# Attention over cached pages: plain float32 matmuls in column quarters in place of split operands

## Chip, cores and metric

The kernel runs on one core of a Trainium2 chip. The metric is the device time of one execution in microseconds (us), lower is better.

## The reference

One inference step of a two-layer decoder: layer 0 is a causal pooling mixer, layer 1 an attention with forget gates. It runs for a prompt (1 x 1024 rows) and for 8 sample sequences of 4 new rows with 2048 past rows in a paged cache (16 pages of 128 rows each). Width 1024, 16 heads of 64. The part that matters here is the sample group's attention:

```python
k_all = jnp.concatenate([past[0], k_new], axis=1)      # 2048 cached rows + 4 new
v_all = jnp.concatenate([past[1], v_new], axis=1)
F_all = jnp.cumsum(lf_all, axis=1)
s = jnp.einsum('bqhd,bkhd->bhqk', q, k_all) * (HEAD_DIM ** -0.5)
s = s + (fq[..., :, None] - fk[..., None, :])          # forget bias, per head
s = jnp.where(mask, s, NEG)
p = jax.nn.softmax(s, axis=-1)
o = jnp.einsum('bhqk,bkhd->bqhd', p, v_all)
```

Everything is float32.

## The kernel before

`build` runs stages with a barrier between them: conditioning, pooling, two output and residual stages, projections, then `stage_attention` (from L1130), and an output and residual stage. Only `stage_attention` changes. In it each engine has its own program, and semaphores order them.

**Steps.** TensorE, ScalarE, VectorE and GpSimd all loop over `for s in range(STEPS)`, with 151 steps. Three streams of work run side by side in a step:
- Prompt attention, one unit a step for steps 0 to 127: one head and one block of 128 queries (`scores` L1394, `turn_probs` L1407, `values` L1414), with VectorE's `logits`, `row_max`, `normalise` and ScalarE's `exps` between. The number of key blocks, 1 to 8, alternates short and long.
- Pages of K, one a step for steps 0 to 127: `turn_K` (L1423) transposes a page of 128 rows in 8 transposes to PSUM banks 6 and 7. Every second step `page_scores` (L1432) takes two pages. A batch has 16 pages, so 8 batches take 128 steps.
- Pages of V, one a step from step V0 = 22 on, to step 149: `page_values` (L1452). The last 22 pages are a tail in which the other two streams have ended.

Side work (`side`, L1471) comes once a batch of 16 steps at fixed steps (`side_work` L1210, L1201): prompt output transposes, transposes of the sample probabilities (`PTd`, `PTn`), and the transposes of the sample output. It uses bank 6 as `turn_K` does, so the next `turn_K` waits until it is read.

**Splits.** A plain float32 matmul costs TensorE more passes than one on fp32r data, so K, V, the queries and the probabilities of the cached pages are split into a high part (cast to fp32r) and the rest. K is split on its way out of PSUM: ScalarE casts (L1561), VectorE subtracts (L1694). V is split in SBUF: ScalarE casts (L1555), GpSimd or, late, VectorE subtracts (L1276). The 64 rows of a batch (16 heads x 4 queries) stand twice in the 128 stationary columns, high and low:

```python
pe.matmul(out, E_all[:, bq, :], G[:, 2 * g * P:2 * (g + 1) * P], start=True, stop=False)
for c in range(NP):
    for kt in (KTh, KTl):
        mm = pe.matmul(out, qst[:, bq % 2, c * P:(c + 1) * P], kt[:, j % 2, c, :], ...)
```

The first matmul (L1440) adds the forget bias `G` by a selector. ScalarE then copies the low rows (L1548) and VectorE adds both halves (L1673). Output bank 3 is shared with `values`, so `page_scores` and `values` wait for each other's readers (L1513, L1522). For V the same is done in L1465 to L1468, with 512 columns a matmul, into banks 4 and 5; L1486 sums and transposes the result by `J`.

**Loads.** SP issues all loads in one list sorted by due time (L1246): pages of K into a ring of 3, of V into a ring of 2 (at the end also into the buffers of K), and for each pair of heads of the prompt qT, kT, zT and Vt. SP waits in order.

**Start.** GpSimd clears and builds masks (L1334 to L1361), VectorE computes the cumulated forget values (L1627) and `G` (L1630); TensorE's first step waits for `newT` and `nmask` (L1501).

Of the kernel before, what the change touches and what calls it, by code (L numbers as in the profile page):

```python
# [59 lines left out]
KR = 3  # L60
VR = 2
# [72 lines left out]
def build(nc, x_prompt, x_sample, state_pool, cache_k, cache_v, cache_logf, page_table, c_prompt,  # L134
# [53 lines left out]
    negF_d = scratch("negF_d", (NH, SEQ))  # L188

# [940 lines left out]
    def stage_attention():  # L1130
# [7 lines left out]
        KTh = a.take("KTh", [P, 2, NP, 2 * P], F32R)  # L1138
        KTl = a.take("KTl", [P, 2, NP, 2 * P], F32R)
        KT_end = a.at  # L1140
        Vh = a.take("Vh", [P, VR, D], F32R)
        Vl = a.take("Vl", [P, VR, D], F32R)
# [20 lines left out]
        QW = P + 2 * NT  # L1163
        qst = a.take("qst", [P, 2, NP * QW], F32R)
        newT = a.take("newT", [NS, NB, NP, 2 * NT])
        Sd = a.take("Sd", [NR, 2, PAST + NS])
        Slo = a.take("Slo", [NR, 2 * P])
        PTd = a.take("PTd", [P, NPG, 2 * NR], F32R)
        PTn = a.take("PTn", [NS, 2 * NR])
        O_sb = a.take("O_sb", [P, D])  # L1170
        J = a.take("J", [P, 3 * NR])
        E_all = a.take("E_all", [P, NB, P])
        G = a.take("Gf", [P, PAST + NS])
        nmask = a.take("nmask", [NR, 2 * NS - NT])
        dstat = a.take("dstat", [NR, 2, 4])
        zero = a.take("zero", [P, 1])
# [14 lines left out]
        mpre = b.take("mpre", [NR, NH, 2 * NS - NT])  # L1191
# [9 lines left out]
        G_OUT, G_PTD, G_PTN, G_PTD2, G_OS = (2, 3), 4, 5, 7, 6  # L1201
# [8 lines left out]
        def side_work(s):  # L1210
# [6 lines left out]
            if g in (G_PTD, G_PTN, G_PTD2) and r < NB:  # L1217
                return "probs", r, (G_PTD, G_PTN, G_PTD2).index(g)
# [9 lines left out]
        s_VK = [sem(f"s_VK{i}") for i in range(KR)]  # L1228
# [5 lines left out]
        s_Kt, s_Kh, s_Kl, s_sc, s_Slo, s_rowe = (sem(n) for n in ("s_Kt", "s_Kh", "s_Kl", "s_sc", "s_Slo", "s_rowe"))  # L1234
        s_Vh, s_Vl = sem("s_Vh"), [sem(f"s_Vl{i}") for i in range(VR)]
        s_qs, s_side_hi, s_ogd = sem("s_qs"), sem("s_side_hi"), [sem(f"s_ogd{i}") for i in range(2)]
# [16 lines left out]
        for p in range(NP):  # L1253
            loads.append((UN * p + 3.8 if p else -9.0, "nF", 2 * p + 1))
        loads.sort()

        TAIL = PAGES - V0
        rest = [(K, x % KR) for x in range(PAGES - KR, PAGES)] + [(V, (TAIL + x) % VR) for x in range(VR)]  # L1260
        places, last, landed = [], {("K", x % KR): ("K", x) for x in range(PAGES - KR, PAGES)}, {}
        for t in range(PAGES):
            buf, i = (V, t % VR) if t < TAIL else rest[(t - TAIL) % len(rest)]
            key = ("K" if buf is K else "V", i)
            landed[key] = landed.get(key, 0) + 16
            places.append((buf[:, i], s_V[i] if buf is V else s_VK[i], landed[key], last.get(key)))
            last[key] = ("V", t)

        def dve_splits(t):

            return t + V0 - 1 >= NU

        def V_low(eng, t):

            eng.wait_ge(s_Vh, t + 1)
            eng.tensor_tensor(Vl[:, t % VR], places[t][0], Vh[:, t % VR].bitcast(F32), ALU.subtract).then_inc(  # L1276
                s_Vl[t % VR], 1)

        with nc.Block() as block:
            @block.sync  # L1280
            def _(sp):
                def pair_loads(p):
# [8 lines left out]
                    sp.dma_start(Vt[:, i], vp[:, :, p * P:(p + 1) * P]).then_inc(s_pair[i], 16)  # L1291

# [17 lines left out]
                for _, what, t in loads:  # L1310
                    if what == "pair":
                        pair_loads(t)
                    elif what == "nF":
                        head_load(t)
                    elif what == "K":
                        if t >= KR:
# [473 lines left out]
```

## Time and profile before

| what | us |
|---|---|
| median of 3 runs | 2380.86 |
| lowest, highest | 2380.86, 2383.38 |
| span of the profiled execution | 2378.0 |
| attention stage in it, first unit's step to last page value | 1379 to 2211 |

The profiled execution's own device time is not given beside its span; its instructions fill 2378.0 us, and the median of the runs is 2.9 us above that. In the rows further down PE is TensorE's matmul, PEld its weight load, DVE VectorE, ACT ScalarE, POOL GpSimd, SPq the queue of SyncE. "L1443" is a line of the kernel before, "x8" a count. A record is one instruction as the trace has it; the ends of matmuls are modelled, so that distances between starts say more than durations.

### The profile page before, as it was taken

The numbers are of one execution on the slowest core, as the hardware profiler recorded it, in microseconds if no ns is written. First come the engines' busy times: TensorE is split into PE (matmuls) and PEld (weight loads), VectorE is DVE, ScalarE is ACT, GpSimd is POOL, SyncE is SP. The second block draws the span as 40 slices with busy tenths as digits, with TensorE's granted clock in tenths as the row PEclk, the third lists the DMA queues.
The fourth block names the chain that finished last, engine by engine and source line by source line (L and its number), as shares of the span: only waits on it lengthen the run. The fifth ranks groups of instructions, "written<-read, shape, count | busy, mean of one in ns | idle before, by whom it ended". The sixth has DMA issues, their size and how long they took to land. (4 is left out here: it accounts for less than half of the span.)

```text
span 2378.0 us, 33033 instructions
## 1 busy us (share of the span) xinstructions
PE 2125.1 (89%) x12939; PEld 1865.5 (78%) x12939; DVE 906.3 (38%) x1510; ACT 763.2 (32%) x1459; POOL 693.5 (29%) x512
## 2 busy tenths in 40 slices
PE   6969999999799924999999889999999999997692
PEld 1269999999799913999999867778788787876692
DVE  1332333344310066210000166555665655655305
ACT  2111111111212133100001135666666656655332
POOL 0123222333122214222233200444444444441122
PEclk9989999999899955999999889999999999999896
DMA  8621212121421041343333243665656656555404
GB/s 282 220 71 40 83 48 82 49 81 50 175 88 45 18 166 30 110 112 93 84 99 97 87 165 119 227 220 186 213 184 226 213 193 213 187 184 189 143 20 166
DMA packets 231052, 312.81 MB, mean 132 GB/s; under 512 B 39777, under 2 KB 165330, under 8 KB 230779
## 3 DMA queue, kind: packets, MB, share of 16 engines
q1 hardware_dynamic: 199251, 266.13, 34.9%
q10 hardware_dynamic: 31520, 44.50, 5.3%
q8 instruction: 103, 1.69, 0.3%
q14 instruction: 50, 0.41, 0.1%
q0 software_dynamic: 128, 0.07, 0.0%
HBM read 266.09 MB, written 44.57 MB: 131 GB/s over the span
## 5 line engine op out<-in xcount | busy, mean ns | idle before, releaser
L1276 POOL TENSOR_TENSOR Vl<-V,Vh 128x1024 fp32r<-128x1024 f32 x106 | 251.9, 2377 | 2.5 <-ACT Vh L1555 2.5
L121 PE MATMUL ps<-actH,w_hi_a 128*128 128x352 f32 x960 | 210.4, 327 | 3.4 <-DVE w_lo_a L92 3.4
L121 PE MATMUL ps<-actH,w_lo_a 128*128 128x352 f32 x960 | 207.8, 324 | 0.0
L121 PE MATMUL ps<-actL,w_hi_a 128*128 128x352 f32 x960 | 207.4, 324 | 0.0
L121 PE MATMUL ps<-actH,w_hi_c 128*128 128x352 f32 x792 | 173.3, 327 | 20.9 <-DVE w_lo_c L92 20.9
L1694 DVE TENSOR_TENSOR KTl<-ps,KTh 128x512 fp32r<-128x512 f32 x256 | 164.5, 685 | 54.3 <-ACT KTh L1561 52.7
L121 PE MATMUL ps<-actH,w_lo_c 128*128 128x352 f32 x792 | 171.5, 324 | 0.0
L121 PE MATMUL ps<-actL,w_hi_c 128*128 128x352 f32 x792 | 171.4, 325 | 0.0
L121 PEld LDWEIGHTS ps<-actH,w_hi_a 128*128 128x128 f32 x960 | 163.4, 190 | 3.8 <-DVE w_lo_a L92 3.7
L1561 ACT CAST KTh<-ps 128x512 fp32r<-128x512 f32 x256 | 137.4, 588 | 89.5 <-PE ps L1428 86.9
L121 PEld LDWEIGHTS ps<-actH,w_lo_a 128*128 128x128 f32 x960 | 165.5, 189 | 0.0
L121 PEld LDWEIGHTS ps<-actL,w_hi_a 128*128 128x128 f32 x960 | 163.7, 189 | 0.0
L1403 PE MATMUL ps<-kT,qT 64*128 64x512 f32 (+3 forms) x384 | 159.6, 523 | 4.1 <-DMA Vt<-out_dram 1.7
L1428 PEld LDWEIGHTS ps<-ident,K 128*128 128x128 f32 x1024 | 111.6, 142 | 64.5 <-issue 44.2
L121 PEld LDWEIGHTS ps<-actH,w_hi_c 128*128 128x128 f32 x792 | 134.8, 190 | 21.0 <-DVE w_lo_c L92 21.0
L1428 PE MATMUL ps<-ident,K 128*128 128x128 f32 x1024 | 142.3, 283 | 6.8 <-DVE newT L1641 4.6
L107 POOL CAST w_hi_a<-w_raw_a 128x1024 fp32r<-128x1024 f32 (+1 forms) x47 | 43.2, 920 | 333.3 <-PE ps L121 324.4
L1443 PE MATMUL ps<-KTh,qst 128*128 128x256 f32 x512 | 137.1, 306 | 0.0
L121 PEld LDWEIGHTS ps<-actH,w_lo_c 128*128 128x128 f32 x792 | 136.7, 189 | 0.0
L121 PEld LDWEIGHTS ps<-actL,w_hi_c 128*128 128x128 f32 x792 | 135.2, 189 | 0.0
L1443 PE MATMUL ps<-KTl,qst 128*128 128x256 f32 x512 | 124.8, 282 | 0.0
L1555 ACT CAST Vh<-V 128x1024 fp32r<-128x1024 f32 x114 | 118.7, 1041 | 9.0 <-PE ps L1467 8.9
(267 smaller groups left out, 3833.8 us busy)
## 6 DMA issues: line engine op xcount, KB each, us to landing
K<-in_cache_k_dram SPq DMA_DIRECT2D x128, 512.0 KB, 3.3
V<-in_cache_v_dram SPq DMA_DIRECT2D x114, 512.0 KB, 3.4
adaw<-in_ada_w_dram SPq DMA_DIRECT2D x12, 2048.0 KB, 8.5
w_raw_a<-in_a_in_w_dram SPq DMA_DIRECT2D x32, 512.0 KB
g_d<-g ACTq DMA_DIRECT2D x16, 528.0 KB, 2.7
mov_b<-g_d SPq DMA_DIRECT2D x16, 528.0 KB, 5.8
w_raw_b<-in_a_out_w_dram SPq DMA_DIRECT2D x16, 512.0 KB
w_raw_c<-in_kv_w_dram SPq DMA_DIRECT2D x16, 512.0 KB
```

The lines of the kernel that those rows point to most:

```text
L107: pool.tensor_copy(hi, raw).then_inc(w["hi_ready"], 1)
L121: mm = pe.matmul(acc[:, c, 0:CH], wt[:, j % SPL, k, :], act[:, k0 + k, c * CH:(c + 1) * CH], start=first and k == 0 and s == 0, stop=last ...
L1276: eng.tensor_tensor(Vl[:, t % VR], places[t][0], Vh[:, t % VR].bitcast(F32), ALU.subtract).then_inc(s_Vl[t % VR], 1)
L1403: mm = pe.matmul(bank[:, c:e], qT[hs, p % 2, i * P:(i + 1) * P], kT[hs, p % 2, c:e], start=True, stop=True)
L1428: mm = pe.transpose(ps[:, 6 + c // 4, c % 4 * P:(c % 4 + 1) * P], K[:, t % KR, c * P:(c + 1) * P], ident[:, :])
L1443: mm = pe.matmul(out, qst[:, bq % 2, c * P:(c + 1) * P], kt[:, j % 2, c, :], start=False, stop=(c == NP - 1 and kt is KTl))
L1555: act.copy(Vh[:, t % VR], src).then_inc(s_Vh, 1)
L1561: act.copy(KTh[:, s // 2 % 2, 4 * h:4 * h + 4, s % 2 * P:(s % 2 + 1) * P], ps[:, 6 + h, :].rearrange("p (c n) -> p c n", c=4)).then_inc(s_ ...
L1694: dve.tensor_tensor(KTl[:, s // 2 % 2, at[0], at[1]], ps[:, 6 + h, :].rearrange("p (c n) -> p c n", c=4), KTh[:, s // 2 % 2, at[0], at[1]] ...
```

## The change

K and V pages are used as plain float32, and there is no split. A batch's queries are laid out in 4 groups of 32 columns: quarter n of the array's columns holds two pairs of heads (16 columns used of 32). `page_scores` issues 8 matmuls of 128 rows by 32 columns over 256 moving columns, two into each quarter, to partitions 32n of bank 5. `page_values` issues 4 matmuls a page, one a quarter, each over the 256 columns of V that belong to the quarter's four heads, to bank 4. K leaves PSUM in two copies at once, by ScalarE (bank 6) and VectorE (bank 7). The forget bias is written to DRAM (`G_d`, four copies, one for each query) and read back into `Fr` in the layout of the score rows; VectorE adds it. The rows of a batch now spread over 128 partitions, with 64 of them unused. The transposes of the probabilities come as four side works of 4 transposes of 128 instead of two of 8 of 64. The rings have 4 buffers each, and V's is released by the matmuls. The sample output is transposed by 2 transposes instead of 8 matmuls by `J`.

```diff
-KR = 3
-VR = 2
+KR = 4
+VR = 4
+QD = 32
...
+    G_d = scratch("G_d", (NB * NH, NT, PAST + NS))
...
-        G_OUT, G_PTD, G_PTN, G_PTD2, G_OS = (2, 3), 4, 5, 7, 6
+        G_OUT, G_PTD, G_PTN, G_OS = (2, 3), (4, 7, 8, 9), 5, 6
...
+        for bq in range(2, NB):
+            loads.append((UN * (bq - 1) + 4.2, "Fr", bq))
...
+                def row_bias(bq):
+                    if bq >= 2:
+                        sp.wait_ge(s_rowe, NPG // 2 * (bq - 1))
+                    for j in range(NQ):
+                        h0 = bq * NH + j * NT
+                        dst = Fr[j * QD:j * QD + NT * NT, bq % 2, :]
+                        src = G_d[h0:h0 + NT].rearrange("h t n -> (h t) n")
+                        sp.dma_start(dst, src).then_inc(s_Fr[bq % 2], 16)
...
-                for _, what, t in loads:
+                started = False
+                for at, what, t in loads:
+                    if at >= 0 and not started:
+                        started = True
+                        sp.wait_ge(s_Gready, 2)
+                        for q in range(NT):
+                            sp.dma_start(G_d[:, q, :], G[:, :]).then_inc(s_Gd, 16)
+                        sp.wait_ge(s_Gd, 16 * NT)
+                        sp.wait_ge(s_Fz, 1)
+                        row_bias(0)
+                        row_bias(1)
...
+                        if t >= VR:
+                            sp.wait_ge(s_pv, t - VR + 1)
+                        sp.dma_start(V[:, t % VR], v_rows[page(t)].rearrange("a k n -> (a k) n")).then_inc(
+                            s_V[t % VR], 16)
...
-                pool.memset(zero[:, :], 0.0).then_inc(s_ones, 1)
-                pool.memset(PTn[:, :], 0.0).then_inc(s_ones, 1)
+                pool.memset(newT[:, :, :, :], 0.0).then_inc(s_ones, 1)
+                pool.memset(qst[:, :, :, :], 0.0).then_inc(s_qz, 1)
...
-                pool.memset(E_all[:, :, :], 0.0).then_inc(s_ones, 1)
                 pool.memset(mpre[:, :, :], 1.0).then_inc(s_ones, 1)
-                pool.wait_ge(s_ones, 7)
+                pool.memset(Fr[:, :, :], 0.0).then_inc(s_Fz, 1)
+                pool.wait_ge(s_ones, 5)
...
-                    if 0 <= s + 1 - V0 < PAGES and not dve_splits(s + 1 - V0):
-                        V_low(pool, s + 1 - V0)
...
-                    out = ps[:, 3, P:3 * P]
-                    pe.matmul(out, E_all[:, bq, :], G[:, 2 * g * P:2 * (g + 1) * P], start=True, stop=False)
-                    for c in range(NP):
-                        for kt in (KTh, KTl):
-                            mm = pe.matmul(out, qst[:, bq % 2, c * P:(c + 1) * P], kt[:, j % 2, c, :],
-                                           start=False, stop=(c == NP - 1 and kt is KTl))
+                    for e in range(2):
+                        for n in range(NQ):
+                            mm = pe.matmul(ps[n * QD:(n + 1) * QD, 5, 0:2 * P], qst[:, bq % 2, 2 * n + e, :],
+                                           KT[:, j % 2, 2 * n + e, :], start=(e == 0), stop=(e == 1))
...
-                    for v in (Vh, Vl):
-                        for c in range(2):
-                            mm = pe.matmul(ps[:, 4 + c, :], PTd[:, g, :], v[:, t % VR, c * BANK:(c + 1) * BANK],
-                                           start=False, stop=(g == NPG - 1 and v is Vl))
+                    for q, c in tile:
+                        mm = pe.matmul(ps[q, 4, 0:HQ], PTd[:, g, q], V[:, t % VR, c], start=False, stop=(g == NPG - 1))
...
-                        for c in range(NP):
-                            mm = pe.matmul(ps[:, 6, 8 * c:8 * c + P], O_sb[:, c * P:(c + 1) * P],
-                                           J[:, 8 * c:8 * c + P], start=True, stop=True)
+                        for e in range(2):
+                            mm = pe.transpose(ps[:, 6, e * P:(e + 1) * P], O_sb[:, e * P:(e + 1) * P], ident[:, :])
...
-                        pe.wait_ge(s_On, s - 1)
                         page_scores(s // 2 - 1)
...
-                        act.copy(Slo[:, :], ps[NR:P, 3, P:3 * P]).then_inc(s_Slo, 1)
...
-                        act.copy(Vh[:, t % VR], src).then_inc(s_Vh, 1)
...
-                        for h in range(2):
-                            act.copy(KTh[:, s // 2 % 2, 4 * h:4 * h + 4, s % 2 * P:(s % 2 + 1) * P],
-                                     ps[:, 6 + h, :].rearrange("p (c n) -> p c n", c=4)).then_inc(s_Kh, 1)
+                        act.copy(KT[:, s // 2 % 2, 0:4, s % 2 * P:(s % 2 + 1) * P],
+                                 ps[:, 6, :].rearrange("p (c n) -> p c n", c=4)).then_inc(s_Kact, 1)
...
-                    mm = dve.tensor_tensor(Sd[:, bq % 2, 2 * g * P:2 * (g + 1) * P], ps[0:NR, 3, P:3 * P], Slo[:, :],
-                                           ALU.add)
+                    if g == 0:
+                        dve.wait_ge(s_Fr[bq % 2], 16 * NQ * (bq // 2 + 1))
+                        link(dve, dve.tensor_tensor(new, new, nmask[:, NS - NT - NT * bq:2 * NS - NT - NT * bq], ALU.add))
+                    dve.wait_ge(s_sc, j + 1)
...
+                    mm = dve.tensor_tensor(Sd[:, bq % 2, c], ps[:, 5, 0:2 * P], Fr[:, bq % 2, c], ALU.add)
```

## Rows read from the trace of the kernel before

**Rows 1.** The page, part 1: busy us, share of the span, instructions.

```profile
PE 2125.1 (89%) x12939; PEld 1865.5 (78%) x12939; DVE 906.3 (38%) x1510; ACT 763.2 (32%) x1459; POOL 693.5 (29%) x512
```

**Rows 2.** Windows: us; PE, PEld, DVE, ACT, POOL busy us; clock; DMA share; GB/s.

```profile
1490.00:2085.00 595.00, 593.04 (x3867) 474.36 (x3866) 349.59 (x693) 370.35 (x659) 253.22 (x192) 1.00 0.61 207
...
2157.00:2213.00 56.00, 38.10 (x171) 26.11 (x170) 31.03 (x32) 26.25 (x28) 0.00 (x0) 0.94 0.52 175
```

**Rows 3.** Groups of TensorE from 1600 to 1900 us.

```profile
L1428 PE MATMUL ps<-ident,K 128*128 128x128 f32 x384 | 52.5, 280 | 0.6 <-DVE ogp L1724 0.6
```

**Rows 4.** Timeline, one even and one odd step: start us, us, what, count.

```profile
2084.86 0.71 PE L1494 MATMUL ps<-ident,Sd 64*128 64x64 f32 x8
...
2086.28 0.28 PE L1443 MATMUL ps<-KTh,qst 128*128 128x256 f32 x1
2086.28 0.19 PEld L1443 LDWEIGHTS ps<-KTl,qst 128*128 128x128 f32 x1
...
2087.84 0.28 PE L1443 MATMUL ps<-KTl,qst 128*128 128x256 f32 x1
...
2088.05 1.12 PE L1403 MATMUL ps<-kT,qT 64*128 64x512 f32 x2
...
2089.10 1.09 PE L1428 MATMUL ps<-ident,K 128*128 128x128 f32 x8
...
2092.17 0.71 PE L1467 MATMUL ps<-Vh,PTd 128*128 128x512 f32 x2
...
2092.72 0.63 PE L1467 MATMUL ps<-Vl,PTd 128*128 128x512 f32 x2
...
2093.27 0.09 PEld L1489 LDWEIGHTS ps<-ident,Sd 64*32 64x32 f32 x1 [0.36 <-issue]
2093.28 0.23 PE L1489 MATMUL ps<-ident,Sd 64*32 64x64 f32 x1
```

**Rows 5.** Timeline, weight loads of one unit's 1024 score columns.

```profile
1388.67 0.19 PEld L1403 LDWEIGHTS ps<-kT,qT 64*128 64x128 f32 x1 [0.24 <-issue]
1389.10 0.19 PEld L1403 LDWEIGHTS ps<-kT,qT 64*128 64x128 f32 x1 [0.24 <-issue]
```

**Rows 6.** Waits of the weight loads, 1490 to 2085 us: total, times, longest.

```profile
PEld ps L1403 <- issue: 35.1, 132, 0.4
PEld ps L1428 <- issue: 32.7, 60, 0.8
...
PEld ps L1428 <- DVE PTd L1728: 4.5, 6, 0.8
...
PEld ps L1479 <- DVE KTl L1694: 2.7, 6, 0.5
```

**Rows 7.** VectorE's groups by form: halves of K, page rows; busy, mean ns, idle.

```profile
L1694 DVE TENSOR_TENSOR KTl<-ps,KTh 128x512 fp32r<-128x512 f32 x256 | 164.5, 685 | 54.3 <-ACT KTh L1561 52.7
...
L1673 DVE TENSOR_TENSOR Sd<-ps,Slo 64x256 f32<-64x256 f32 x64 | 26.7, 417 | 120.6 <-ACT Slo L1548 120.6
```

**Rows 8.** Timelines of the stage's start: GpSimd, VectorE, TensorE.

```profile
1358.92 0.94 POOL L1339 MEMSET E_all<- 128x1024 f32 x1
...
1366.42 2.20 DVE L1613 TENSOR_TENSOR J<-ident 128x64 f32<-128x64 f32 x3
...
1376.05 1.87 DVE L1638 TENSOR_REDUCE nmask<-mpre 64x60 f32<-64x960 f32 x1
...
1401.34 1.09 PE L1428 MATMUL ps<-ident,K 128*128 128x128 f32 x8
```

**Rows 9.** The page, part 2: what the DMA engines moved, in 40 slices.

```profile
GB/s 282 220 71 40 83 48 82 49 81 50 175 88 45 18 166 30 110 112 93 84 99 97 87 165 119 227 220 186 213 184 226 213 193 213 187 184 189 143 20 166
```

**Rows 10.** TensorE's timeline at the stage's end.

```profile
2205.24 0.73 PE L1467 MATMUL ps<-Vh,PTd 128*128 128x512 f32 x2 [1.32 <-DVE Vl L1276]
...
2208.89 0.74 PE L1467 MATMUL ps<-Vh,PTd 128*128 128x512 f32 x2 [1.33 <-DVE Vl L1276]
...
2211.28 2.02 PE L1486 MATMUL ps<-J,O_sb 128*128 128x128 f32 x16 [1.19 <-ACT O_sb L1585]
```

More of the change, by code:

```diff
@@ L1137, in stage_attention @@
         KT_at = a.at
[L1138 to L1139 removed]
+        KT = a.take("KT", [P, 2, NP, 2 * P])
+        Sd = a.take("Sd", [P, 2, PAST + NS])
         KT_end = a.at
[L1141 to L1142 removed]
         qT = a.take("qT", [P, 2, SEQ])
@@ L1160, in stage_attention @@
         qblk = a.take("qblk", [P, NP, NB, 2 * NT])
[L1163 to L1172, printed above, removed]
+        NQ = P // QD
+        HQ = D // NQ
+        qst = a.take("qst", [P, 2, NP, QD])
+        newT = a.take("newT", [NS, NB, NQ, QD])
+        Fr = a.take("Fr", [P, 2, PAST + NS])
+        PTd = a.take("PTd", [P, NPG, P])
+        PTn = a.take("PTn", [NS, P])
+        O_sb = a.take("O_sb", [P, HQ])
         G = a.take("Gf", [P, PAST + NS])
-        nmask = a.take("nmask", [NR, 2 * NS - NT])
-        dstat = a.take("dstat", [NR, 2, 4])
-        zero = a.take("zero", [P, 1])
+        nmask = a.take("nmask", [P, 2 * NS - NT])
+        dstat = a.take("dstat", [P, 2, 4])
         ogp = a.take("ogp", [P, 2, SEQ])
@@ L1190, in stage_attention @@
         one = b.take("one", [P, 1])
-        mpre = b.take("mpre", [NR, NH, 2 * NS - NT])
+        mpre = b.take("mpre", [P, P // NT, 2 * NS - NT])
         assert b.at <= KT_end
@@ L1216, in side_work @@
                 return "out", r, G_OUT.index(g)
-            if g in (G_PTD, G_PTN, G_PTD2) and r < NB:
-                return "probs", r, (G_PTD, G_PTN, G_PTD2).index(g)
+            if g == G_PTN and r < NB:
+                return "new probs", r, 0
+            if g in G_PTD and r < NB:
+                return "probs", r, G_PTD.index(g)
             if g == G_OS and 1 <= r <= NB:
@@ L1227, in stage_attention @@
         s_V = [sem(f"s_V{i}") for i in range(VR)]
-        s_VK = [sem(f"s_VK{i}") for i in range(KR)]
+        s_Fr = [sem(f"s_Fr{i}") for i in range(2)]
         s_c, s_ones = sem("s_cst5"), sem("s_ones5")
@@ L1454, in page_values @@
                     bq, g = t // NPG, t % NPG
-                    pe.wait_ge(s_Vl[t % VR], t // VR + 1)
+                    pe.wait_ge(s_V[t % VR], 16 * (t // VR + 1))
+                    tile = [(slice(n * QD, (n + 1) * QD), slice(n * HQ, (n + 1) * HQ)) for n in range(NQ)]
                     if g == 0:
@@ L1611, in _ @@
                                     q_s[r, :, :].rearrange("p k (b t) -> p k b t", t=NT)).then_inc(s_qst, 1)
-                for i in range(3):
-                    dve.tensor_tensor(J[:, i * NR:(i + 1) * NR], ident[:, 0:NR], ident[:, NR:P], ALU.add)
                 def queries(bq):
@@ L1640, in _ @@
                 dve.wait_ge(s_nT, 1)
-                dve.tensor_copy(newT[:, :, :, :].rearrange("n b k c -> n k b c"),
-                                ps[0:NS, 5, :].rearrange("n (k b c) -> n k b c", k=NP, b=NB)).then_inc(s_newT, 1)
+                n5 = ps[0:NS, 5, :].rearrange("n (j e b c) -> n j e b c", j=NQ, e=2, b=NB)
+                for e in range(2):
+                    dve.tensor_copy(newT[:, :, :, 2 * NT * e:2 * NT * (e + 1)].rearrange("n b j c -> n j b c"),
+                                    n5[:, :, e]).then_inc(s_newT, 1)
                 def logits(u):
```

162 lines of the change are left out of this document (59 added, 103 removed).

## The prediction

> **What bounds the kernel now.** I read the totals first [rows 1]: TensorE is busy 89% of 2378.0 us, VectorE 38%, ScalarE 32%, GpSimd 29%. Busy shares average over stages, so the stretches of the attention stage come next [rows 2]. From 1490 to 2085 us TensorE is busy 593 of 595 us at a granted clock of 1.00, VectorE 350, ScalarE 370, the DMA engines 0.61. So in the middle of the stage only TensorE's own stream counts; the splits of K and V on ScalarE, VectorE and GpSimd that the change drops are covered. Of 128 steps, those of 1600 to 1900 us take 300/48 = 6.25 us each (384 page transposes, 8 a step [rows 3]). At the stage's end [rows 2] it is different: TensorE is busy 38 of 56 us.
>
> Next I need start-to-start distances, not busy times, since matmuls overlap.
> - A matmul on split (fp32r) data is one record: 0.12 us apart with 256 columns [rows 4] (13 distances from 2086.28 to 2087.84; I use 0.118). With 512 columns, two of Vh then two of Vl, I take 0.215 each, twice the columns less the fixed part (2092.17 to 2092.72 is 0.55 for two, with the edges) [rows 4].
> - A plain float32 matmul is two records. With 512 columns the weight loads stand 0.43 apart [rows 5]: 0.43 a record, 0.216 with 256 columns, so 0.432 for a whole 256-column matmul. Plain float32 costs nearly four times a split pass.
> - A transpose of 128 columns: 8 in 1.09 us; less the 0.27 that one takes alone and over 7 distances, 0.117 each. Of 64 rows: 8 in 0.71, one alone 0.23: 0.067 each [rows 4].
> - Going to 64-row matmuls and back costs idle weight loads. Scores at 2088.05 need 2 x 0.43 = 0.86, the next transpose starts 1.05 later, 0.09 was lost on the way in: 0.28 for both ways, **0.14 a switch** [rows 4]. The list of waits shows the same [rows 6]: "issue" ahead of L1403 and L1428, 68 us in 595.
>
> **The unknown price: how the four quarters overlap.** No row of this trace has two matmuls in different column quarters, so it is bounded. Each quarter matmul has two records on the same quarter, issued one behind the other. From above: nothing overlaps, 0.432 us a matmul. From below: only the issue limits, two records of 0.067 us (the shortest distance of a loaded matmul here [rows 4]), 0.134. I take the value between that the order of issue gives: the second record must wait for its own quarter, and what is queued behind waits with it; then the next quarter's first record runs beside it. So a matmul starts every **0.216 us** and a group of n takes (n+1) x 0.216. A quarter's weight load must be early for this; in full-width matmuls it starts with the matmul before it (load and matmul both at 2086.28 [rows 4]).
>
> The rule that speaks against this: the Trainium skill, "TensorE: Matmul & The Clock Gate", Part 3, "The mechanism", says that a weight load overlaps matmuls in flight only when its row group differs from theirs; the quarters share all rows. The trace disagrees for full width, where load and matmul do overlap. By the rule the sum would be that of the late loads among the rivals, 2470 us; by the row it is the forecast.
>
> **Part by part, in TensorE time.**
> 1. Pairs of pages with both scores and values (53 of 64 pairs; values start 22 steps late). Before: 2 x 0.216 for the bias (L1440) + 16 x 0.118 + 8 x 0.215 = 4.04 us. After: the even step runs values and scores back to back, 12 matmuls, 13 x 0.216; the odd step 4, 5 x 0.216: 3.89. Saved 0.15. But each step now enters the quarter mode from full width, one switch more, 2 x 0.14. Net +0.13 x 53 = **+7**.
> 2. The first 11 pairs, scores alone: 9 x 0.216 = 1.94 against 2.32, +0.14: **-3**.
> 3. Side work (8 batches) now sits in full-width mode between quarter groups: on 4 even steps a batch the group breaks in two, 4 x 0.216 x 8 = **+7**; about 9 further switches a batch (side work of before switches too, for 64-row transposes and L1461), 9 x 0.14 x 8 = **+10**.
> 4. Side work itself, a batch: L1486 16 records to 2 transposes, -14 x 0.117 = -1.64; L1461 4 x 0.43 to 4 quarters at 0.216, -0.86; probability transposes 16 x 0.117 against 16 x 0.067, +0.80; bias matmul of the new columns -0.15. -1.85 x 8 = **-15**.
> 5. Waits on evacuations. Now TensorE waits for K's low half (KTl) or for VectorE's second half of PTd: 2.7 + 4.5 = 7 us in 595 [rows 6], 9 over the stage. K now takes two casts on ScalarE and behind each a subtraction of 0.69 us on VectorE [rows 7]; then each engine copies one half, side by side. PTd is left to ScalarE alone, but four times a batch. I take two thirds of the 9: **-6** (bounds -9 and +3, for the four evacuations). Dropping the copy of the low rows, the V casts and splits, and the wait for o_tok ahead of L1440 is worth nothing more: TensorE's stream covers them, and VectorE's new bias add keeps the 256 columns of L1673 (0.42 us [rows 7]).
> 6. Stage start. GpSimd's clears ahead of bm grow: Fr, 4160 columns at 0.94 us per 1024 [rows 8] is 3.8, mpre grows by 960 (+0.9), newT and qst for E_all, +0.5: X, which waits for bm, starts 5.2 later. VectorE drops J (-2.2) and its mask reduction doubles (+1.9): step 0 comes about 5 us later. Then SP waits, and its queue with it: four writes of G, 4.26 MB, 15 us at the best rate of the page (282 GB/s [rows 9]), 22 at 190, then 8 loads into Fr, and behind them the load of page 4. G, complete before the mask reduction at 1376.05 [rows 8], is ready near 1379; page 4 would land near 1403 to 1410, and is wanted near 1406 (step 4 began at 1401.3 [rows 8]): 0 to 6 us, I take 2. VectorE's page rows at step 3 wait for the same. **+7** (bounds +3 and +15). The six later Fr loads sit behind waits long met: nothing; if that cover goes, it is their issue, 4 x 0.4 us.
> 7. Tail, 22 pages of values alone. Before, two pages take 3.65 us behind VectorE's split (1.3 us idle [rows 10]), 51 us in all. After, no split; the bound becomes the load of V: 0.52 MB at 282 GB/s is 1.86 us a page, no faster than 1.83. What goes is the slow beginning of the tail and part of the prefetched pages: **-8** (bounds -14 and 0). The last evacuation and the 16 records of L1486 shrink [rows 10]: **-2**.
>
> Sum: +7 -3 +7 +10 -15 -6 +7 -8 -2 = -3 us. The profiled span is 2378.0; the median of the three runs is 2380.9, taken as the same execution plus 2.9 us around it. Forecast **2378 us**.
>
> All hangs on one term: 64 x 8 + 128 x 4 = 1024 quarter matmuls, so 0.01 us in the distance is 10 us in the time. The break-even with before is a distance of 0.219 us.
>
> **Rivals.**
> - Full overlap: records of different quarters pass those that wait. An even step then takes 22 x 0.067 + 0.43 = 1.9 us instead of 2.8, an odd one 0.83 instead of 1.08: -1.16 x 53 - 6 = -67, or 2311; with no issue limit the twelve matmuls of an even step take 6 x 0.216 and the four of an odd one 0.43, at most -2.16 x 53 - 12 = -126, 2252. I put it at 2300. For it: ScalarE and VectorE have room; a step time of 5.2 to 5.7 us stays above what they need, and the DMA share would be near 0.7. Against: two records in turn on one quarter. The Trainium skill, "TensorEngine Tiling (Array Packing)", section "Key Properties", says that tiles load and multiply in parallel; that is this case, and no row here shows it. Chance 0.27.
> - Late loads, the other side: a quarter's weight load starts only when the matmul before it does not stream, and adds its 0.09 us (the 32-column load of L1489 [rows 4]) to each matmul: 0.306. 1024 x 0.09 = +92, **2470**. Every 0.01 us of it is 10 us, so it decides from 0.008 us of added load upwards. Chance 0.14.
> - The quarters don't run at once at all: 0.432, less the group ends that I counted (some 30 us): +190, **2570**. Speaks against: quarters use different columns. Chance 0.14.
>
> **Numbers.** My forecast 0.45, its own range 2355 to 2400 (bounds of items 5 to 7 and +-0.01 us of distance). What a measurement of this kernel can tell is 0.2%, about 5 us; within the forecast I give 0.19 faster, 0.09 the same, 0.17 slower. With the rivals: faster 0.27 + 0.19 = 0.46; same 0.09; slower 0.14 + 0.14 + 0.17 = 0.45. The range runs from most of the full overlap to the late loads, 2265 to 2470, and leaves out the serial case and the best of the full overlap.
>
> **What would show it.** In the new profile: starts of the quarter matmuls' records. Forecast: pairs of records with nearly one start, 0.216 us from pair to pair, 5 records' time for a page's values. All eight within 0.6 us: full overlap. Each 0.216 behind the last with no overlap: serial; 0.3 a matmul: late loads. Idle "issue" time of 0.14 at each entry and exit. Step 0 some 5 us later, a gap near step 3 or 4 behind Fr or K. The tail near 1.9 us a page behind V's DMA. A granted clock below 1.00 in the middle would break every term.

## The result: 6.4% faster, 148 us below the forecast

| | before | after |
|---|---|---|
| median, us | 2382.05 (4 runs, 2380.86 to 2383.38) | 2230.24 (3 runs, 2227.76 to 2231.38) |
| span of the profiled execution, us | 2378.0 | 2229.6 |
| mean granted clock | 0.951 | 0.942 |
| ratio, 95% interval | | 0.936, 0.9345 to 0.9375 |

A fourth run of the changed kernel took 7072.3 us and is left out. The forecast was 2378 us and the range 2265 to 2470, so the result lies below the range too. The mechanism is that of the rival called full overlap, which was priced at 2300, with 2252 as its limit.

Part 1 of the page after, which answers to [rows 1]:

```profile
PE 1975.7 (89%) x13227; PEld 1666.3 (75%) x13227; DVE 800.2 (36%) x1367; ACT 565.4 (25%) x1155; POOL 443.4 (20%) x403
```

TensorE has 288 more records and is busy 149 us less, and the span is 148 us less. Its share of the span is 89% as before. The windows after answer to [rows 2] (us; PE, PEld, DVE, ACT, POOL busy us; clock; DMA share; GB/s):

```profile
1490.00:1970.00 480.00, 478.41 (x4071) 327.49 (x4072) 285.03 (x597) 222.83 (x427) 27.78 (x95) 1.00 0.78 259
...
2026.00:2070.00 44.00, 24.24 (x188) 7.50 (x186) 5.26 (x13) 5.36 (x9) 0.00 (x0) 0.64 0.66 220
```

In the middle TensorE is busy 478.4 of 480 us at a clock of 1.00: it still bounds, with a shorter stream. The DMA share rose from 0.61 to 0.78, because a page is used up faster; by its share that is the nearest other limit. ScalarE fell from 62% of this stretch to 46%, GpSimd from 43% to 6%, and none of that shows in the time, as an experiment below confirms.

TensorE's timeline after, parts of two even steps and of an odd one, answers to [rows 4]:

```profile
1803.09 0.66 PE L1480 MATMUL ps<-ident,Sd 128*128 128x128 f32 x4
1803.68 1.07 PE L1435 MATMUL ps<-KT,qst 128*32 128x256 f32 x16
...
1807.32 1.73 PE L1409 MATMUL ps<-Vt,PT_long 128*128 128x128 f32 x14
1808.98 0.64 PE L1456 MATMUL ps<-V,PTd 128*32 128x256 f32 x8
1809.55 0.28 PE L1475 MATMUL ps<-ident,Sd 128*32 128x128 f32 x1
...
2005.78 0.64 PE L1456 MATMUL ps<-V,PTd 128*32 128x256 f32 x8
2006.23 1.05 PE L1435 MATMUL ps<-KT,qst 128*32 128x256 f32 x16
2007.21 1.12 PE L1393 MATMUL ps<-kT,qT 64*128 64x512 f32 x2
```

From start to start the 16 records of `page_scores` take 0.98 us; before, L1440 and L1443 took 2088.05 - 2085.50 = 2.55 us. The 8 records of `page_values` take 0.57 us (1808.98 to 1809.55) where another array mode (another split of the array into rows and columns) follows, and 0.45 where scores follow in the same mode; before it was 1.10 (2092.17 to 2093.27 [rows 4]). A pair of steps with both is 1.43 + 0.57 = 2.00 us now. The way into the mode costs 0.02 us behind the 14 records of L1409 (1.66 us to the next start, 14 x 0.117 = 1.64) and 0.12 behind the four transposes of L1480 (0.59 against 0.47); the way out is 0.57 - 0.43 = 0.14.

How that comes about can be counted in windows of a few hundredths of a microsecond, for the records of L1456 alone (us; PE busy, records running; PEld the same; clock; DMA share; GB/s):

```profile
1808.95:1809.00 0.05, 0.02 (x4) 0.03 (x4) 1.00 0.40 164
...
1809.15:1809.20 0.05, 0.05 (x4) 0.00 (x0) 1.00 1.39 573
1809.20:1809.25 0.05, 0.05 (x8) 0.00 (x0) 1.00 0.60 246
```

Four records have started by 1809.00, within 0.02 us of 1808.98. The view counts records and does not name their quarter; that there is one in each is inferred, since at full width two such records take turns (full_width_scores below). Four run until 1809.20; then the other four start: 8 are counted while one set ends and the next begins. So eight records are two rounds of 0.216 us, and a quarter matmul costs 0.432/4 = **0.108 us**, not 0.216. The even step is 24 records in 6 rounds: 6 x 0.216 = 1.30, with 0.13 for the way out of the mode 1.43, as measured.

The stage's start. TensorE's timeline, step 0 before, then steps 0 and 4 after, and SyncE's queue after (same columns):

```profile
1378.79 1.97 PE L1428 MATMUL ps<-ident,K 128*128 128x128 f32 x8 [4.59 <-DVE newT L1641]
```

```profile
1384.18 1.97 PE L1419 MATMUL ps<-ident,K 128*128 128x128 f32 x8 [5.66 <-DVE newT L1607]
...
1406.45 1.09 PE L1419 MATMUL ps<-ident,K 128*128 128x128 f32 x8
```

```profile
1379.58 3.06 SPq L1306 DMA_DIRECT2D G_d<-Gf  x4
1391.09 3.56 SPq L1281 DMA_DIRECT2D Fr<-G_d  x8
```

Step 0 starts at 1384.18 instead of 1378.79, and step 4 at 1406.45 instead of 1401.34 [rows 8]: both 5 us late, so nothing was lost in between. The four writes of `G_d` (4.26 MB) were done when SP went on at 1391.09, 11.5 us after the first was issued.

The stage's end answers to [rows 10]:

```profile
2058.12 1.08 PE L1456 MATMUL ps<-V,PTd 128*32 128x256 f32 x8 [2.98 <-DMA V<-in_cache_v_dram]
...
2061.92 1.08 PE L1456 MATMUL ps<-V,PTd 128*32 128x256 f32 x8 [0.17 <-DMA V<-in_cache_v_dram]
```

The wait behind VectorE's split is gone and a wait for the load of V has come, 9.2 us over the tail. The clock is 0.64 in that window, after TensorE had idled almost half of it: eight records take 1.08 us there instead of 0.64.

**The sum.** Each span is cut at the K transposes of step 0, those of step 127, and the end of the attention stage.

| stretch | before | after | difference |
|---|---|---|---|
| up to step 0 | 1378.8 | 1384.2 | +5.4 |
| step 0 to step 127 | 771.6 | 632.7 | -138.9 |
| step 127 to the end of the stage | 63.4 | 47.6 | -15.8 |
| the stage behind | 164.3 | 165.1 | +0.8 |
| span | 2378.0 | 2229.6 | -148.4 |

In the middle, steps 48 to 64, sixteen steps take 80.9 us instead of 99.9, 2.4 us less for each pair of steps. This distance, from one K transpose to another within one trace at a clock of 1.00, is also the sharpest measure for the experiments.

### The profile page after: what moved, and what is told of

Its sections match the earlier page's. It is cut to its first block and busy times, and to the rows that moved or that the text cites. A ratio compares the mean times of both kernels' runs of the same rounds, so it can differ in the third digit from the quotient of the medians.

```text
span 2229.6 us, 33182 instructions
## 1 busy us (share of the span) xinstructions
PE 1975.7 (89%) x13227; PEld 1666.3 (75%) x13227; DVE 800.2 (36%) x1367; ACT 565.4 (25%) x1155; POOL 443.4 (20%) x403
## 5 line engine op out<-in xcount | busy, mean ns | idle before, releaser
L1393 PE MATMUL ps<-kT,qT 64*128 64x512 f32 (+3 forms) x384 | 161.6, 529 | 1.7 <-ACT PT_long L1537 1.1
L1393 PEld LDWEIGHTS ps<-kT,qT 64*128 64x128 f32 x384 | 62.9, 189 | 74.1 <-issue 67.7
L756 DVE COPY y_tok<-ps 128x512 f32<-128x512 f32 (+1 forms) x48 | 23.6, 547 | 255.1 <-PE ps L746 255.1
L1530 ACT COPY KT<-ps 128x512 f32<-128x512 f32 x128 | 74.7, 584 | 153.4 <-PE ps L1419 153.4
L1409 PE MATMUL ps<-Vt,PT_long 128*128 128x128 f32 x832 | 103.5, 275 | 0.0
L122 PE MATMUL ps<-actH,w_hi_b 128*128 128x352 f32 x384 | 84.9, 329 | 17.8 <-DVE actL L843 16.3
L724 DVE SCALAR_TENSOR_TENSOR g<-ps,asc,sz 128x1056 f32<-128x1056 f32 x16 | 21.1, 1318 | 221.2 <-PE ps L122 221.2
```

Of the source, the lines that this page charges most:

```text
L122: mm = pe.matmul(acc[:, c, 0:CH], wt[:, j % SPL, k, :], act[:, k0 + k, c * CH:(c + 1) * CH], start=first and k == 0 and s == 0, stop=last ...
L724: dve.scalar_tensor_tensor(out=as_thirds(g[:, j % 2]), in0=thirds(acc[n % 2]), scalar=asc[:, j:j + 1], in1=as_thirds(sz[:, j % 2]), op0=AL ...
L756: dve.tensor_copy(dst[0:r, tiles[0]:tiles[-1] + 1, :], ps[0:r, bank, 0:len(tiles) * P].rearrange("p (i n) -> p i n", n=P)).then_inc(self.r ...
L1393: mm = pe.matmul(bank[:, c:e], qT[hs, p % 2, i * P:(i + 1) * P], kT[hs, p % 2, c:e], start=True, stop=True)
L1409: mm = pe.matmul(ps[:, 3, 0:P], PT[u % 4][:, j * P:(j + 1) * P], Vt[:, p % 2, j, :], start=(j == 0), stop=(j == i))
L1530: act.copy(KT[:, s // 2 % 2, 0:4, s % 2 * P:(s % 2 + 1) * P], ps[:, 6, :].rearrange("p (c n) -> p c n", c=4)).then_inc(s_Kact, 1)
```

## The experiments

The theory that the first group tests (A): records of different quarters pass one that waits, four quarters run as four arrays, and TensorE's stream sets the time. The runs came in four groups, each beside runs of the kernel before (medians 2380.94, 2381.24, 2382.94 and 2381.81 us). The changed kernel itself was timed only at first, so differences against its 2230.2 carry some 3 us; ratios are against the kernel before. All diffs are against the changed kernel.

**1. The order of issue (inner_pairs).** If a record that waits held back what is queued behind it, the order of the loops would matter most.

```diff
-                    for e in range(2):
-                        for n in range(NQ):
+                    for n in range(NQ):
+                        for e in range(2):
```

> page_scores with the loops exchanged: both matmuls of a quarter follow one another (n outer, e inner), so that four records in a row go to one quarter. Theory A (records pass others that wait for a busy quarter, as if each quarter had its own queue): page_scores stays 1.0 us, time 2230 +-4. Theory B (issue stops at the first matmul whose quarter is busy; the overlap seen in the changed kernel comes from four matmuls in a row on four quarters): the group takes 5 x 0.43 = 2.16 us instead of 0.87, +83 us, 2313.

Measured: 2229.68 us, ratio 0.9362 (0.9346 to 0.9377): no change. Steps 48 to 64 take 81.15 us instead of 80.94, so the order costs about 0.03 us a group. Two cuts of 0.02 us at the beginning of the group, for L1435 alone, first with the pairs inside:

```profile
2006.49:2006.51 0.02, 0.02 (x2) 0.02 (x2) 1.00 0.50 205
2006.51:2006.53 0.02, 0.02 (x4) 0.02 (x5) 1.00 0.82 205
```

and in the changed kernel:

```profile
2006.23:2006.25 0.02, 0.02 (x3) 0.01 (x3) 1.00 1.78 205
2006.25:2006.27 0.02, 0.02 (x4) 0.02 (x4) 1.00 1.59 205
```

With pairs inside, four records in turn go to one quarter, and only 2 records have started after 0.02 us instead of 3; but soon four records run at once. The whole group takes 1.02 us and not 2.16:

```profile
2006.49 1.08 PE L1435 MATMUL ps<-KT,qst 128*32 128x256 f32 x16
2007.51 1.12 PE L1393 MATMUL ps<-kT,qT 64*128 64x512 f32 x2
```

So the first record of the next quarter does not wait until the three ahead of it in the program have started, each 0.216 us behind the last. What this shows is that at least four records of one quarter can wait without holding back the others; more were not tried. The Trainium skill, "TensorE: Matmul & The Clock Gate", Part 3, "The mechanism", has matmuls start strictly in program order; the starts in this trace do not agree, and the group's 1.02 us confirms them. Its rule that a weight load overlaps only with another row group would have shown as the late loads; here the quarters share all rows and PEld runs beside PE. The same section has an exception to that rule, loads into the background weight buffer, which this trace would fit.

**2. Plain float32 without quarters (full_width_scores).** The queries stand at their own 32 columns of a 128-column stationary operand, the other columns are zero, and 8 matmuls over the full width give the same scores.

```diff
...
-                    for e in range(2):
-                        for n in range(NQ):
-                            mm = pe.matmul(ps[n * QD:(n + 1) * QD, 5, 0:2 * P], qst[:, bq % 2, 2 * n + e, :],
-                                           KT[:, j % 2, 2 * n + e, :], start=(e == 0), stop=(e == 1))
+                    for c in range(NP):
+                        mm = pe.matmul(ps[:, 5, 0:2 * P], qst[:, bq % 2, c, :], KT[:, j % 2, c, :],
+                                       start=(c == 0), stop=(c == NP - 1))
...
```

> Scores as 8 plain float32 matmuls with all 128 stationary columns (the queries of a pair of heads in their 8 columns, zeros elsewhere), values left in quarters. Price of one full-width 256-column matmul 0.432 us, so 3.46 + 0.1 us a pair of pages instead of 1.0: +2.55 x 64 = +163, less two mode switches on some steps (-5): 2388. If the quarters were worth less than their overlap suggests (another engine already the bound), the loss is under 120.

Measured: 2391.60 us, ratio 1.0043 (1.0026 to 1.006), +162 us against inner_pairs in the same group. Its timeline:

```profile
2110.88 3.62 PE L1434 MATMUL ps<-KT,qst 128*128 128x256 f32 x16
2114.43 1.12 PE L1393 MATMUL ps<-kT,qT 64*128 64x512 f32 x2
```

The same 16 records take 3.55 us instead of 0.98. 2.57 x 64 = 164 us, and 162 came. The whole gain and more hangs on the overlap: with the scores alone at full width the change is 0.4% slower than the kernel before, by an interval that just excludes equality.

**3. Values in halves (values_in_halves).** Two matmuls of 64 columns over 512 moving columns in place of four of 32 over 256.

```diff
-                    tile = [(slice(n * QD, (n + 1) * QD), slice(n * HQ, (n + 1) * HQ)) for n in range(NQ)]
+                    tile = [(slice(n * 2 * QD, (n + 1) * 2 * QD), slice(n * 2 * HQ, (n + 1) * 2 * HQ)) for n in range(2)]
...
-                        mm = pe.matmul(ps[q, 4, 0:HQ], PTd[:, g, q], V[:, t % VR, c], start=False, stop=(g == NPG - 1))
+                        mm = pe.matmul(ps[q, 4, :], PTd[:, g, q], V[:, t % VR, c], start=False, stop=(g == NPG - 1))
...
```

> Values in two halves of 64 columns with 512 moving columns each (half of the output block is not used) instead of four quarters with 256. If halves overlap two by two: 2 records x 0.43 = 0.86 us a page instead of 0.43, +0.43 x 106 pages beside the prompt units = +46, the 22 of the tail are hidden behind the loads: 2276. If halves don't overlap: 1.72 us, +137 on the 106 pages: 2367.

Measured: 2281.54 us, ratio 0.9585 (0.9569 to 0.9601), +52 against inner_pairs. Its timeline:

```profile
2012.29 1.08 PE L1456 MATMUL ps<-V,PTd 128*64 128x512 f32 x4
2013.30 0.28 PE L1475 MATMUL ps<-ident,Sd 128*32 128x128 f32 x1
```

1.01 us for two rounds of 0.43 and the way out (0.14): halves overlap two by two. 0.44 us more a page, for the 106 pages ahead of the tail, is 47. The matmuls of the new columns (L1452) are in halves too: 1.00 us against 0.56, once in each of 8 batches, which is 3.5 of the other 5. The rest, near the spread between runs, was not separated.

**4. One more round (zero_round).** Four quarter matmuls with a zero stationary operand ahead of each group of scores: 8 records, they add nothing to the sums.

```diff
+                    for n in range(NQ):
+                        pe.matmul(ps[n * QD:(n + 1) * QD, 5, 0:2 * P], zq[:, :], KT[:, j % 2, 2 * n, :],
+                                  start=True, stop=False)
...
-                                           KT[:, j % 2, 2 * n + e, :], start=(e == 0), stop=(e == 1))
+                                           KT[:, j % 2, 2 * n + e, :], start=False, stop=(e == 1))
...
```

> Four more quarter matmuls ahead of each page_scores, with a stationary of zeros, so that the scores stay as they are: what the forget bias would cost TensorE if it stayed there, in quarters. Theory that TensorE alone bounds the 128 steps: 2 rounds x 0.216 x 64 = +28 us, 2259. Theory that a chain over VectorE and ScalarE or the loads (DMA share 0.78) have begun to bound: under +14.

Measured: 2251.87 us, ratio 0.9457 (0.9442 to 0.9473), +22 against inner_pairs. Its timeline:

```profile
2016.57 0.61 PE L1439 MATMUL ps<-KT,zq 128*32 128x256 f32 x8
2017.00 1.05 PE L1443 MATMUL ps<-KT,qst 128*32 128x256 f32 x16
```

The added records take 0.43 us each time, 27.5 in 64 groups, and four fifths show. In steps 48 to 64 nearly all of it shows: 84.3 us instead of 80.9, 3.3 for eight groups of 0.43. So TensorE sets the time of the steps there; which steps hide the other 5 us is open.

**5 to 8. What is left in the changed kernel.** Three small edits, each alone and then together: GpSimd clears `Fr` after its masks (clear_Fr_last), the side work comes before `page_values`, so that values and scores are not parted by it (side_before_values), and the last 22 pages of V use the buffers of K too (tail_in_K_buffers).

**clear_Fr_last.**

```diff
-                pool.memset(Fr[:, :, :], 0.0).then_inc(s_Fz, 1)
...
+                pool.memset(Fr[:, :, :], 0.0).then_inc(s_Fz, 1)
```

> GpSimd clears Fr (3.56 us) behind its masks instead of ahead of them. If that clear is what delays step 0 (first page transpose at 1384.2 instead of 1378.8 us), step 0 comes 3.6 us earlier and the time falls by 3.6 us to 2226.5. If VectorE's longer mask reduction and its share of the SBUF port with GpSimd are what counts, under 1 us.

Measured: 2226.43 us, ratio 0.9346 (0.9333 to 0.9359). The number was met, but step 0 did not come earlier. Starts in two profiles can't be compared as they stand, since the stages ahead take up to 4 us more or less from one profile to the next. GpSimd's first clear of this stage marks its beginning, in the changed kernel, here, and in three_together (below), which has the same edit:

```profile
1358.26 0.52 POOL L1332 MEMSET qblk<- 128x512 f32 x1 [27.02 <-POOLq L176]
1361.21 0.53 POOL L1332 MEMSET qblk<- 128x512 f32 x1 [27.02 <-POOLq L176]
1360.90 0.52 POOL L1342 MEMSET qblk<- 128x512 f32 x1 [27.22 <-POOLq L176]
```

Step 0 starts 25.9 us behind that clear in the changed kernel (1384.18), 26.0 here (1387.25), and 22.5 in three_together (1383.43). VectorE's timeline, in the changed kernel:

```profile
1366.18 2.06 DVE L1571 TENSOR_TENSOR X<-bm,lf_s 32x128 f32<-32x128 f32 x1 [11.84 <-POOL bm L1344]
...
1368.29 4.12 DVE L1578 COPY qblk<-q_s 64x256 f32<-64x256 f32 x2
1372.45 4.43 DVE L1591 TENSOR_TENSOR_SCAN Fs<-one,LT 128x2052 f32<-128x2052 f32 x1
```

and here:

```profile
1367.85 7.63 DVE L1579 COPY qblk<-q_s 64x256 f32<-64x256 f32 x2
1375.51 4.43 DVE L1592 TENSOR_TENSOR_SCAN Fs<-one,LT 128x2052 f32<-128x2052 f32 x1
```

and in three_together:

```profile
1367.54 4.12 DVE L1590 COPY qblk<-q_s 64x256 f32<-64x256 f32 x2
```

The two small copies end with GpSimd's work: in the changed kernel at 1372.4 with its mask selections (1372.3), here at 1375.5 with the clear of `Fr` (1371.77 and 3.56 us), but in three_together at 1371.7, again with the selections (1371.5), though the same clear follows. There the edit brings step 0 the 3.4 us that were expected; here it brings nothing. Why the copies outlast the selections in one profile and not in the other is open.

Here step 4 began at 1406.29, 45.1 us behind the first clear and not 48.2, at a clock of 0.83 from 1384 to 1412 us against 0.71 in the changed kernel. That is not the edit: inner_pairs and side_before_values, with the start of the changed kernel, have 45.1 and 44.8. And 4 us is near what differs between groups of runs: no gain is shown for this edit alone.

**side_before_values.**

```diff
+                    if side_work(s):
+                        side(s, *side_work(s))
                     if V0 <= s < V0 + PAGES:
                         page_values(s - V0)
-                    if side_work(s):
-                        side(s, *side_work(s))
```

> Side work ahead of page_values instead of between page_values and page_scores, so that TensorE enters and leaves the quarter mode once a step. Switches as priced by the changed kernel's timeline (0.12 us for values to side, 0.12 us for side to scores on an even step, some 0.1 on an odd one): 1.4 us a batch, 11 us in all, 2219. If the side work's inputs come later than that, its waits eat it: no gain or a loss.

Measured: 2223.61 us, ratio 0.9337 (0.9324 to 0.935), -7. Steps 48 to 64, one batch, take 80.0 us instead of 80.9, which makes 7 in 8 batches. Waits of the weight loads, 1490 to 2000 us, in the changed kernel (total, times, longest):

```profile
PEld ps L1480 <- issue: 11.1, 27, 0.4
PEld ps L1456 <- issue: 10.2, 51, 0.4
...
PEld ps L1435 <- issue: 4.2, 25, 0.2
```

and with the side work ahead:

```profile
PEld ps L1393 <- issue: 64.2, 198, 0.4
...
PEld ps L1456 <- issue: 14.6, 77, 0.4
```

The waits at L1480 and L1435, which each way in and out of the quarter mode had left, are gone. Some of it comes back at L1456 and L1393 (10.2 and 56.0 before), where the switches now are; the window also holds a little more of the stream.

**tail_in_K_buffers.**

```diff
...
-                        sp.dma_start(V[:, t % VR], v_rows[page(t)].rearrange("a k n -> (a k) n")).then_inc(
-                            s_V[t % VR], 16)
+                        dst, signal, _, old = places[t]
+                        if old:
+                            sp.wait_ge(s_pv if old[0] == "V" else s_Kt, old[1] + 1)
+                        sp.dma_start(dst, v_rows[page(t)].rearrange("a k n -> (a k) n")).then_inc(signal, 16)
...
```

> The last 22 pages of V may also use K's four buffers, as in the kernel before. In the tail TensorE now waits for V's DMA (9.2 us in all). Four more pages can be on their way before the tail begins, when the DMA engines are busy 0.59: 4 x 1.8 = 7 us, 2223. If the DMA engines are what bounds already ahead of the tail: under 2 us.

Measured: 2223.05 us, ratio 0.9336 (0.9323 to 0.9348), -7: most of the 9.2 us of waits in the tail. The intervals of these single edits touch that of the changed kernel; that of the three together (**three_together**) does not:

> The three edits in one kernel. If they are independent their gains add: 3.6 + 11 + 7 = 22 us, 2208. The shorter steps may leave the loads less time, so 12 to 22 us.

Measured: 2214.39 us, ratio 0.9292 (0.928 to 0.9305), 16 us below the changed kernel.

**9. The larger rings (rings_3_and_2).** Dropping the splits freed the memory for them, so their part was taken back alone.

```diff
-KR = 4
-VR = 4
+KR = 3
+VR = 2
```

> The rings of the kernel before, 3 pages of K and 2 of V, all else as changed. V's load of page t is now released by the matmuls of page t-2, one step of 4.95 us ahead of its use, and takes 4.2 us to land behind up to one K load. If the deeper rings carry part of the gain: TensorE waits for V on many steps, +30 to +130 us, 2260 to 2360. If two buffers were enough: under 5 us, 2230 to 2236.

Measured: 2261.84 us, ratio 0.9497 (0.9481 to 0.9513), +32. The window and the next-to-last page of the tail:

```profile
1490.00:1970.00 480.00, 469.37 (x3987) 320.80 (x3985) 278.38 (x585) 216.29 (x418) 27.18 (x93) 1.00 0.77 256
```

```profile
2087.14 1.08 PE L1456 MATMUL ps<-V,PTd 128*32 128x256 f32 x8 [1.55 <-DMA V<-in_cache_v_dram]
```

TensorE idles 10.6 of 480 us instead of 1.6, step 3 waits 4.0 us for K, and most of the last twenty pages wait, from 2057 us on nearly all of them, 1.0 to 1.65 us each. Of the 27 us that the span grew, 14 lie between step 0 and step 127, the 4.0 among them, and 13 behind step 127, in the tail. So the deeper rings are worth at most a fifth of the gain. At most, because this tail has two buffers for V, and that of the kernel before had those of K besides, which the run does not give back.

**10. The engines that were relieved (split_work_kept).** ScalarE copies and GpSimd subtracts 128 x 1024 elements in each of 106 steps, on data that nothing reads.

```diff
...
+                        pool.tensor_tensor(Vy[:, :], Vx[:, (s + 1 - V0) % 2, :], Vx[:, (s + 1 - V0) % 2, :],
+                                           ALU.subtract).then_inc(s_Vy, 1)
...
+                        act.copy(Vx[:, (s + 1 - V0) % 2, :], G[:, 0:D]).then_inc(s_Vx, 1)
...
```

> For 106 pages ScalarE makes again a 128x1024 copy ahead of its half of K, and GpSimd a 128x1024 subtraction behind it, on other data, so that TensorE waits for neither: the work of the V split without its dependence. If TensorE's stream covers the other engines, as the prediction said: 0 to +6 us, 2230 to 2236. If the shorter steps had made ScalarE's chain (K, probabilities, exponentials) the next bound: 106 x up to 1.05, +30 to +110.

Measured: 2230.46 us, ratio 0.9365 (0.9349 to 0.9381): nothing lost. Its window:

```profile
1490.00:1970.00 480.00, 475.54 (x4035) 325.60 (x4029) 286.21 (x594) 305.37 (x520) 204.28 (x189) 1.00 0.77 258
```

ScalarE is busy 305 instead of 223 us and GpSimd 204 instead of 28. The work that the change takes from them was worth nothing in itself; VectorE's share of the splits was not put back.

**11. The start (start_reordered).** GpSimd's mask selections wait until VectorE's copies to `qblk` are done, and `Fr` is cleared after `G` is ready.

```diff
-                pool.memset(Fr[:, :, :], 0.0).then_inc(s_Fz, 1)
...
+                pool.wait_ge(s_qst, 2)
...
+                pool.wait_ge(s_Gready, 2)
+                pool.memset(Fr[:, :, :], 0.0).then_inc(s_Fz, 1)
```

> GpSimd starts its mask selections only when VectorE's copies to qblk are done, and clears Fr only when G is complete. Theory: the start is late because VectorE's qblk copies (0.5 us of work each) last until GpSimd's running work ends (in the changed kernel both end at 1372.4, with Fr cleared behind the masks the copies took 7.6 us). Then the scan begins some 5 us earlier and step 0 with it: 1378 to 1379 instead of 1384.2; the time falls by 5 to 6 us to 2224. If something else delays the copies, the scan begins no earlier than 1371.

Measured: 2228.54 us, ratio 0.9348 (0.9335 to 0.9361): -2, within what can't be told apart. GpSimd's timeline, then VectorE's:

```profile
1360.55 0.53 POOL L1332 MEMSET qblk<- 128x512 f32 x1 [27.02 <-POOLq L176]
...
1366.83 6.21 POOL L1348 TENSOR_SCALAR_AFFINE_SELECT mpre<-mpre 128x1920 f32<-128x1920 f32 x1 [1.79 <-DVE qblk L1581]
```

```profile
1366.16 0.61 DVE L1581 COPY qblk<-q_s 64x256 f32<-64x256 f32 x2 [0.68 <-DMA v_s<-out_dram]
1366.79 4.43 DVE L1594 TENSOR_TENSOR_SCAN Fs<-one,LT 128x2052 f32<-128x2052 f32 x1
1371.26 2.86 DVE L1596 TENSOR_SCALAR Fs<-Fs 128x2052 f32<-128x2052 f32 x1
1374.15 2.91 DVE L1597 COPY Gf<-Fs 128x2048 f32<-128x2048 f32 x1
1376.98 1.98 DVE L1598 COPY Gf<-Fs 128x32 f32<-128x32 f32 x1
```

The copies fell from 4.12 to 0.61 us, and counted from GpSimd's first clear the scan began at 6.2 us and not at 14.2. But the same GpSimd selections now lie beside the scan and the copies of `G`: the first takes 6.21 us instead of 2.0, and the three steps behind the scan take 2.86, 2.91 and 1.98 instead of 1.29, 1.23 and 0.17. So `G` is ready at 18.4 us instead of 21.3 and step 0 starts at 23.0 (1383.58) instead of 25.9: of the 8 us 3 are left. The expectation counted what the copies would gain and not what the selections, moved behind them, would cost.

**12. All four edits (four_edits).**

> The start reordered, side work before values, and K's buffers in the tail. three_together gave 2214.4 with a start that came no earlier (step 0 at 1383.4). With 5 us from the start: 2209; if the loads at the start hold it back instead (DMA share 0.81 to 0.91 there): 2213 to 2215.

Measured: 2213.01 us, ratio 0.9289 (0.9276 to 0.9302). That is the fastest kernel here, 7.1% below the one before and 0.8% below the changed one, and no different from the three edits together. The expectation took it that the start of three_together came no earlier, from its absolute time. Counted from the first clear, step 0 starts at 22.5 us there and at 22.7 here (1381.59 - 1358.92), so this start had nothing to add.

## Why the prediction was wrong

**What bounds the kernel** was read rightly: TensorE's stream alone in the middle, before and after (split_work_kept, zero_round). Each price read from a row held: 0.216 us for a float32 record of 256 columns (two rounds of 0.216 in a page of values), 0.43 for one of 512 (values_in_halves), 0.14 us for a way out of a mode (0.57 against 0.43).

**The step that failed** is "The unknown price: how the four quarters overlap". It took a matmul every 0.216 us, because the second record "must wait for its own quarter, and what is queued behind waits with it". What is queued for other quarters does not wait: four records start within 0.02 us, and in inner_pairs another order of issue costs 0.03 us a group and not 1.2. The measured distance is 0.108. For a full pair of steps the prediction had 3.89 us after the change, with the ways in and out 3.89 + 4 x 0.14 = 4.45; the trace has 2.00 and 0.02 to 0.12 for each of two ways in. Before it had 4.04 + 2 x 0.14 = 4.32, and the trace has about 4.6: 2.55 for bias and scores, 1.0 to 1.1 for each page of values. So the term is not +0.13 but near -2.5 a pair, -132 for 53 of them instead of +7, and for the first 11 pairs near -1.5 each, -17 instead of -3. That is -149; -139 arrived. Items 3 to 5, +7 +10 -15 -6 = -4 as predicted, came out near +10. side_before_values finds 7 us of this in the groups that the side work breaks, since those ways in and out end (L1480, L1435). Item 3 had +7 for these groups as well, but by luck: it took it from (n+1) x 0.216, the rule that failed. The rest was not taken apart.

**The second bound failed too**: the floor of the issue, 0.067 us a record, put the rival at 2300. 24 records in 1.30 us are 0.054 each, and with pairs inside the quarters' first records follow each other within hundredths of a microsecond. The 0.067 of the 64-row transposes was therefore no floor for records in quarters. The rival's limit without that floor, 6 x 0.216 + 0.43 = 1.73 us a pair before the switches, is the measured number of rounds; the time is below its 2252 since the kernel before spent more on its pairs than was counted, the ways in cost less than 0.14, and the tail gained more.

**Item 5** (waits on evacuations, -6): the wait for VectorE's `ogp` of 7.3 us remains from 1490 to 2000 us, the others are small. It was not measured alone.

**Item 6** (start, +7): +5.4. Step 0 came 5.4 us late, as predicted. Counted from GpSimd's first clear it is 5.2: X starts 4.5 later, `J` is gone (-2.2), the mask reduction takes 1.7 more, and VectorE's small copies, which end with GpSimd's selections, 4.12 us instead of 2.81, which the item had not. three_together gives 3.4 of it back by clearing `Fr` later. The wait behind the writes of `G` (2 us) did not come: they took 11.5 us and not 15 to 22. The 282 GB/s behind the 15 was the mean of a slice of 59 us, not a rate that the loads can't pass; in the kernel before they move 385 from 10 to 20 us:

```profile
10.00:20.00 10.00, 6.56 (x11) 1.20 (x12) 0.00 (x0) 0.00 (x0) 0.00 (x0) 1.00 1.05 385
```

**Item 7** (tail, -8 and -2): -16. The bound by V's load was right: the pages from 2045 to 2062 us stand 1.8 us apart, where 1.86 was expected. But the four buffers of V, which the item passed over, carry much of the gain (13 us behind step 127 in rings_3_and_2).

**The other rivals.** Late loads (0.306 a matmul) and no overlap (0.432) are both excluded by the 0.108. The rule on weight loads, against which the forecast was set, would have given 2470. full_width_scores shows what it costs where nothing overlaps: 162 us for the scores alone.

**The break-even** was placed at 0.219 us a matmul. full_width_scores has a mean distance of (0.432 + 0.108)/2 = 0.27, and lies 10 us above before; at 10 us for each 0.01 the break-even is near 0.26, since before was costlier than counted. That the result hangs on one unmeasured term had been said. The value taken between the two bounds had no row behind it, and 0.27 for four independent quarters was a low chance for a case that no row spoke against.

## What to carry to other kernels

When the stationary side of a plain float32 matmul fills only a quarter of the columns, try four such matmuls in four column quarters: here they cost what one costs, and beat the exact split into high and low parts. Group them, since each way out of the mode cost 0.14 us here. When one engine's stream is the bound, count nothing for work taken off the others, but count what the freed memory buys in deeper rings. A prediction whose sum hangs on one unseen overlap should give the independent case its full weight, and not a value halfway. And compare starts in two profiles from a mark within the stage, not from the span's beginning: the stages ahead differ by up to 4 us.

## What was not expected of the hardware

- Records of one quarter hold back only their own quarter: four in turn for one (inner_pairs) delay a group of scores by some 0.03 us. 24 records with 24 weight loads run in six rounds of 0.216 us.
- The write of `G_d` moved 4.26 MB in 11.5 us, 370 GB/s, near the 385 of the densest loads of the kernel before.
- VectorE's float32 copies within on-chip memory (SBUF) stretch beside GpSimd's work: the same two copies took 0.61, 4.12 and 7.63 us, and GpSimd's selection 2.0 and 6.21, by what ran beside them. The scan took 4.43 us in each of them, also with a selection beside it; that selection ended 1.8 us behind the scan, about its own 2.0.
- A way into the quarter mode costs 0.02 to 0.12 us, by what is ahead of it, and a way out 0.12 to 0.14.
